# Feed-forward rows of a decoder block: the second norm's scale for the up rows applied at the output, product sums kept in PSUM, and the taps behind them

## What is computed

```python
hf = rmsnorm(x, norm_ffn_g[i])
g_pre = causal_dwconv(hf @ ffn_w_gate[i], ffn_conv_w[i], ffn_conv_b[i])
ff = (jax.nn.gelu(g_pre, approximate=False) * (hf @ ffn_w_up[i])) @ ffn_w_down[i]
x = x + ff
```

## Time and profile before

| | |
|---|---|
| median of 3 runs | 1895.88 us |
| the profiled execution | 1893.21 us |
| its span, first to last instruction | 1891.0 us |
| TensorE busy | 1804.0 us, 95% |
| VectorE busy | 1084.9 us, 57% |
| GpSimd busy | 871.9 us, 46% |
| ScalarE busy | 572.4 us, 30% |
| mean granted clock of TensorE | 0.990 |

### The profile page before, as it was taken

How to read it: one execution, slowest core, us unless ns; L and a number is a source line. 1 busy time by engine, 2 the same in 40 slices (tenths; PEclk the granted TensorE clock), 3 DMA queues, 4 the chain that set the end, 5 groups by cost and what they waited for, 6 DMA issues and landing times.

```text
span 1891.0 us, 24004 instructions
## 1 busy us (share of the span) xinstructions
PE 1804.0 (95%) x8628; PEld 1422.1 (75%) x8628; DVE 1084.9 (57%) x1531; ACT 572.4 (30%) x1095; POOL 871.9 (46%) x597
## 2 busy tenths in 40 slices
PE   7999999999999988999999999999999999999999
PEld 5777677767776766788788878777777777788887
DVE  5346644564654488344311333898888888943534
ACT  5542444344245423112311222523333333200000
POOL 7436443643543274563344433365556555322221
PEclk9999999999999999999999999999999999999999
DMA  4111211211121023445311144221112113145311
GB/s 168 34 40 40 59 49 40 62 51 40 40 56 45 23 68 90 113 112 174 105 67 67 67 167 167 100 101 67 67 67 92 74 67 111 57 177 210 112 44 56
DMA packets 64185, 157.99 MB, mean 84 GB/s; under 512 B 10912, under 2 KB 27680, under 8 KB 64112
## 3 DMA queue, kind: packets, MB, share of 16 engines
q1 hardware_dynamic: 51856, 145.35, 22.7%
q10 hardware_dynamic: 11792, 10.04, 2.0%
q0 software_dynamic: 464, 1.62, 0.2%
HBM read 123.54 MB, written 32.26 MB: 82 GB/s over the span
## 4 chain that ended last, share of the span: by engine, by line
PE 44%; DVE 22%; issue 18%; POOL 10%; ACT 3%; DMA 1%; DVEq 1%; POOLq 0%; SPq 0%; ACTq 0%
PE bank L899 7%; PE bank L900 7%; PE bank L901 7%; PE bank L1317 4%; PE bank L1319 4%; PE bank L1318 4%; POOL wlo L623 3%; DVE cv L2030 2%; PE bank L913 2%; PE bank L1047 2%; PE bank L1060 2%; PE bank L1033 2%; DVE st L2015 2%; DVE gbuf L2082 2%; DVE gbuf L2075 2%
## 5 line engine op out<-in xcount | busy, mean ns | idle before, releaser
L899 PE MATMUL bank<-hhi,whi 128*128 128x512 f32 x1024 | 421.4, 412 | 13.7 <-POOL wlo L623 8.0
L900 PE MATMUL bank<-hlo,whi 128*128 128x512 f32 x1024 | 404.8, 395 | 0.0
L901 PE MATMUL bank<-hhi,wlo 128*128 128x512 f32 x1024 | 404.6, 395 | 0.0
L623 POOL TENSOR_TENSOR wlo<-raw,whi 128x1024 fp32r<-128x1024 f32 (+1 forms) x84 | 196.6, 2340 | 236.6 <-DVE whi L1656 234.7
L899 PEld LDWEIGHTS bank<-hhi,whi 128*128 128x128 f32 x1024 | 193.7, 189 | 63.5 <-POOL wlo L623 10.4
L901 PEld LDWEIGHTS bank<-hhi,wlo 128*128 128x128 f32 x1024 | 193.4, 189 | 45.3
L900 PEld LDWEIGHTS bank<-hlo,whi 128*128 128x128 f32 x1024 | 194.0, 189 | 39.4 <-issue 1.2
L872 POOL TENSOR_TENSOR plo<-st,phi 128x512 fp32r<-128x512 f32 x60 | 108.3, 1819 | 50.2 <-ACT phi L1567 50.2
L1810 DVE CUSTOM_DVE_ANT_0 sp<-bank,mask 128x128 f32<-128x128 f32 (+1 forms) x192 | 56.1, 348 | 121.3 <-PE bank L1033 120.7
L1656 DVE CAST whi<-raw 128x1024 fp32r<-128x1024 f32 (+1 forms) x84 | 69.4, 826 | 93.3 <-PE bank L901 62.0
L1432 ACT ACTIVATE sp<-sp,negm 128x128 f32<-128x128 f32 (+1 forms) x192 | 83.8, 438 | 111.4 <-DVE negm L1814 111.4
(11 more groups left out here) (304 smaller groups left out, 4039.9 us busy)
## 6 DMA issues: line engine op xcount, KB each, us to landing
raw<-in_wblocks SPq DMA_DIRECT2D x98, 512.0 KB, 3.6
pair<-in_wblocks SPq DMA_DIRECT2D x40, 512.0 KB, 4.2
ff_scr<-ffo SPq DMA_DIRECT2D x22, 512.0 KB, 2.8
ff<-ff_scr SPq DMA_DIRECT2D x22, 512.0 KB, 4.1
rt<-rt_scr SPq DMA_DIRECT2D x8, 516.0 KB, 6.7
x<-in_xT SPq DMA_DIRECT2D x8, 512.0 KB, 8.7
zb_scr<-zb SPq DMA_DIRECT2D x8, 512.0 KB, 3.2
zb<-zb_scr SPq DMA_DIRECT2D x8, 512.0 KB, 3.3
```

The costliest lines, as they stand in the source:

```text
L623: pool.tensor_tensor(wlo[par][:, 0:cols], raw[par][:, 0:cols], whi[par][:, 0:cols].bitcast(F32), ALU.subtract).then_inc(lo_done, 1)
L899: nc.tensor.matmul(ps, a, x, start=start and k == k_list[0], stop=False)
L900: nc.tensor.matmul(ps, a, y, start=False, stop=False)
L901: last = nc.tensor.matmul(ps, b, x, start=False, stop=stop and k == k_list[-1])
```

## The change

Of the up rows, the factor rs1 is no longer applied to cv in each unit; each of the 16 output halves is multiplied by rs1 after the down projection, ahead of the residual. The results of four sums (C11, C12, C22, C21) are written back to the banks of the products that they read, and what follows reads them there. ScalarE no longer copies S1. The sums of S3 stand ahead of the taps on VectorE; ScalarE's tap stands behind the casts after S4 and waits for the second gate scaling (N_G1). ffo is made in two halves. TensorE waits for the first gate scaling ahead of A12 and for the whole end of the unit before (ff_done) ahead of S1. The banks of the down projection are taken in another order.

```diff
@@ -59,7 +59,8 @@
 NU = NF - 2
 SLOTS = 7
 I_A11, I_A12, I_S2, I_S1, I_S4, I_S3, I_A22 = range(1, SLOTS + 1)
-N_C11, N_U2, N_V, N_C12, N_U3, N_C22, N_C21 = range(1, SLOTS + 1)
+SUMS = 9
+N_C11, N_U2, N_G0, N_V, N_C12, N_G1, N_U3, N_C22, N_C21 = range(1, SUMS + 1)
 T_2, T_1, T_4, T_3 = range(4)
 B_11, B_12, B_21, B_22 = range(4)
 S_1, S_2, S_4, S_3 = range(4)
@@ -359,7 +360,7 @@
             return cws[:].rearrange("p (a b) c -> p b a c", b=2)[:, p, f2, :]
 
         def dbank(m, h):
-            return bank[(2 * m + h + 3) % 8]
+            return bank[(3, 4, 5, 6, 0, 1, 7, 2)[2 * m + h]]
 
         def half(ap, h):
             return ap[:, h * HT:(h + 1) * HT]
@@ -1274,19 +1275,20 @@
                 if first:
                     pe.wait_ge(ff_done, 2 + 4)
                 else:
-                    pe.wait_ge(copied, 2 * u)
-                    pe.wait_ge(cdone, SLOTS * u - SLOTS + N_C12)
+                    pe.wait_ge(copied, u)
                 product(I_A11, u, of_b(B_11))
+                if not first:
+                    pe.wait_ge(cdone, SUMS * u - SUMS + N_G0)
                 product(I_A12, u, of_b(B_21))
                 if first:
                     pe.wait_ge(tlo_done, KC // 2)
                 product(I_S2, u, of_t(T_2))
+                if not first:
+                    pe.wait_ge(ff_done, 2 * u + 8)
                 product(I_S1, u, of_t(T_1))
                 if first:
                     pe.wait_ge(gs_done, 2)
                 product(I_S4, u, of_b(B_22))
-                if not first:
-                    pe.wait_ge(cdone, SLOTS * u)
                 product(I_S3, u, of_t(T_3))
                 if first:
                     pe.wait_ge(ff_done, 4 + 4)
@@ -1308,10 +1310,11 @@
                             if free and c == 0:
                                 pe.wait_ge(out_ready, 2 * m + h + 1)
                             if start and not free and c == 0 and 2 * m + h == 1:
-                                pe.wait_ge(copied, 2 * NU)
-                                pe.wait_ge(cdone, SLOTS * (NU - 1) + N_C12)
+                                pe.wait_ge(copied, NU)
+                            if start and not free and c == 0 and 2 * m + h == 2:
+                                pe.wait_ge(cdone, SUMS * (NU - 1) + N_U3)
                             if start and not free and c == 0 and 2 * m + h == 6:
-                                pe.wait_ge(cdone, SLOTS * NU)
+                                pe.wait_ge(ff_done, 2 * NF + 4)
                             r = slice(c * HT + m * P, c * HT + (m + 1) * P)
                             x, y, ps = half(fhi[:, c, :], h), half(flo[:, c, :], h), dbank(m, h)[:]
                             nc.tensor.matmul(ps, dhi[par][:, r], x, start=start and c == 0, stop=False)
@@ -1554,7 +1557,6 @@
                 act.activation(thi[:, :, c, :], tbuf[c % 2][:].rearrange("p i (h t) -> p (i h) t", h=2), ACT.Copy).then_inc(thi_done, 1)
 
             def tap(f2, p):
-                act.wait_ge(gs_done, 2 * f2 + p + 1)
                 act.wait_ge(ff_done, 4 * f2 + 2 * p + 4)
                 w = conv_w(f2, p)
                 act.activation(cv[:], gbuf[:, p, 2:], ACT.Identity, scale=w[:, 2:3], bias=w[:, 3:4]).then_inc(tap_done, 1)
@@ -1583,17 +1585,14 @@
 
                 act.wait_ge(prod, SLOTS * u + I_A11)
                 if not first:
-                    act.wait_ge(cdone, SLOTS * u - SLOTS + N_U2)
+                    act.wait_ge(cdone, SUMS * u - SUMS + N_U2)
                 copy(s1_t[:], I_A11)
                 next_cast(I_A11)
                 next_cast(I_A12)
                 next_cast(I_S2)
-                act.wait_ge(prod, SLOTS * u + I_S1)
-                if not first:
-                    act.wait_ge(ff_done, 2 * u + 8)
-                copy(up_t[:, 1], I_S1)
                 next_cast(I_S1)
                 next_cast(I_S4)
+                act.wait_ge(cdone, SUMS * u + N_G1)
                 tap(i2 + 1, p)
                 next_cast(I_S3)
                 gelu(i2 + 1, p)
@@ -1608,6 +1607,7 @@
             rms(rs1, bank[2:4], 2)
             act.add_instruction(mybir.InstLoadActFuncSet(
                 name=nc.get_next_instruction_name(), engine=act.engine, act_func_set_id=GELU_SET))
+            act.wait_ge(gs_done, 1)
             tap(0, 0)
             t_scale(3)
             t_hi(3)
@@ -1617,6 +1617,7 @@
             act.wait_ge(pair_in[1], 32)
             cast(I_A11, 0)
             cast(I_A12, 0)
+            act.wait_ge(gs_done, 2)
             tap(0, 1)
             act.wait_ge(s_added, 4)
             cast(I_S2, 0)
@@ -2025,9 +2026,8 @@
                 link(V.scalar_tensor_tensor(cv[:], gbuf[:, p, 1:T + 1], w[:, 1:2], cv[:], ALU.mult, ALU.add))
                 V.scalar_tensor_tensor(cv[:], gbuf[:, p, 0:T], w[:, 0:1], cv[:], ALU.mult, ALU.add).then_inc(cv_done, 1)
 
-            def scaled(f2, p):
+            def activated(f2, p):
                 dve.wait_ge(gelu_done, 2 * f2 + p + 1)
-                link(TT(cv[:], cv[:], rs1[:], ALU.mult))
                 if not isinstance(f2, int) or f2:
                     dve.wait_ge(ff_out[p], 16 * f2)
 
@@ -2039,7 +2039,7 @@
                 last.then_inc(gs_done, 1)
 
             def up_evict(p):
-                scaled(0, p)
+                activated(0, p)
                 for h in range(2):
                     dve.wait_ge(groups, G_G + 4 * p + 2 + h + 1)
                     TT(half(ffo[p][:], h), half(cv[:], h), fbank(p, 1, h), ALU.mult).then_inc(ff_done, 1)
@@ -2048,14 +2048,19 @@
 
                 u = 2 * i2 + p
                 dve.wait_ge(prod, SLOTS * u + I_A22)
-                dve.wait_ge(cdone, SLOTS * u + N_C22)
-                TT(up_t[:, 0], up_t[:, 0], pbank(I_A22), ALU.add).then_inc(cdone, 1)
-                scaled(i2 + 1, p)
-                dve.wait_ge(cdone, SLOTS * u + N_C21)
-                TT(ffo[p][:], cv[:], up_t[:].rearrange("p h t -> p (h t)"), ALU.mult).then_inc(ff_done, 2)
+                dve.wait_ge(cdone, SUMS * u + N_C22)
+                TT(pbank(I_A22), up_t[:, 0], pbank(I_A22), ALU.add).then_inc(cdone, 1)
+                activated(i2 + 1, p)
+                TT(half(ffo[p][:], 1), half(cv[:], 1), pbank(I_S1), ALU.mult).then_inc(ff_done, 1)
+                dve.wait_ge(cdone, SUMS * u + N_C21)
+                TT(half(ffo[p][:], 0), half(cv[:], 0), pbank(I_A22), ALU.mult).then_inc(ff_done, 1)
 
             def unit(i2, p, first=False, last=False):
                 u = 2 * i2 + p
+
+                def added(n):
+                    dve.wait_ge(cdone, SUMS * u + n)
+
                 g = [gbuf[:, p, 2 + h * HT:2 + (h + 1) * HT] for h in range(2)]
                 if first:
                     up_evict(1)
@@ -2064,34 +2069,34 @@
                 if not last:
                     s_adds(i2 + p, 1 - p)
                 dve.wait_ge(prod, SLOTS * u + I_A12)
-                dve.wait_ge(copied, 2 * u + 1)
-                dve.wait_ge(cv_done, 2 * i2 + p + 1)
-                TT(g[0], s1_t[:], pbank(I_A12), ALU.add).then_inc(cdone, 1)
+                dve.wait_ge(copied, u + 1)
+                TT(pbank(I_A12), s1_t[:], pbank(I_A12), ALU.add).then_inc(cdone, 1)
                 dve.wait_ge(prod, SLOTS * u + I_S2)
                 if not first:
-                    dve.wait_ge(ff_done, 2 * u + 8)
+                    dve.wait_ge(cdone, SUMS * u)
                 TT(up_t[:, 0], s1_t[:], pbank(I_S2), ALU.add).then_inc(cdone, 1)
-                dve.wait_ge(cdone, SLOTS * u + N_C11)
-                link(TT(g[0], g[0], half(rs1[:], 0), ALU.mult))
+                added(N_C11)
+                dve.wait_ge(cv_done, 2 * i2 + p + 1)
+                TT(g[0], pbank(I_A12), half(rs1[:], 0), ALU.mult).then_inc(cdone, 1)
                 if last:
                     dve.wait_ge(ff_in[0], 32)
                     for x in range(2):
                         fsplit(0, 0, x, first=True)
-                dve.wait_ge(copied, 2 * u + 2)
-                dve.wait_ge(cdone, SLOTS * u + N_U2)
-                TT(g[1], up_t[:, 0], up_t[:, 1], ALU.add).then_inc(cdone, 1)
+                dve.wait_ge(prod, SLOTS * u + I_S1)
+                added(N_U2)
+                TT(up_t[:, 1], up_t[:, 0], pbank(I_S1), ALU.add).then_inc(cdone, 1)
                 if last:
                     hi_down(B_D, 0)
                 dve.wait_ge(prod, SLOTS * u + I_S4)
-                dve.wait_ge(cdone, SLOTS * u + N_V)
-                TT(g[1], g[1], pbank(I_S4), ALU.add).then_inc(cdone, 1)
-                dve.wait_ge(cdone, SLOTS * u + N_C12)
-                TT(g[1], g[1], half(rs1[:], 1), ALU.mult).then_inc(gs_done, 1)
-                conv(i2 + 1, p)
+                added(N_V)
+                TT(pbank(I_S4), up_t[:, 1], pbank(I_S4), ALU.add).then_inc(cdone, 1)
+                added(N_C12)
+                TT(g[1], pbank(I_S4), half(rs1[:], 1), ALU.mult).then_inc(cdone, 1)
                 dve.wait_ge(prod, SLOTS * u + I_S3)
```

(11 more changed lines are left out.)

## The result

The changed kernel takes 1864.71 us (median of 4 runs, 1863.58 to 1869.11), against 1895.95 of the kernel before beside it: ratio 0.984, 95% interval 0.982 to 0.9859. Measured again with the experiments it is 1866.34 against 1895.03, ratio 0.9849 (0.9834 to 0.9864). Forecast was 1867.8.

What follows compares the result with a forecast made beforehand. VectorE's loop with its tap wait set the 21.1 us units; after the change TensorE would bound at 19.35. Gains 34.1 + 2.4, losses 5.1 + 3.3: 28.1 us saved, 1867.8 us by the median; 8-in-10 range 1861 to 1882.

Steps and rivals of the forecast that it cites:

- Bound and units: The 20 units: TensorE would bound at 19.35 us each instead of 21.1, gaining 34.1 us in all.
- VectorE's loop: VectorE's work and waits per unit: predicted 17.9 us after the change, under TensorE's 19.35 by 1.4.
- Handoff: From last unit to down projection: the 2.59 us gap at the seventh bank would shrink, gaining 2.36 us, bounds 1.9 to 2.4.
- Evictions: Output halves after the down projection: 1.32 us each instead of 0.60, losing 5.1 us at the end, 3.3 in the middle.
- Sum: Whole kernel: 34.1 + 2.4 us gained, 5.1 + 3.3 lost, a saving of 28.1 us.
- Sums into PSUM: Four VectorE sums per unit that write PSUM banks: taken at 0.69 us each, bounds 0.6 and 1.72.
- rival B: Slower: VectorE sums writing PSUM are dear, 1.72 us each, lengthening the loop to 22.0; 1922 us, chance 0.04.
- cover of 1.4 us: Per unit, the margin by which VectorE's predicted 17.9 us stays under TensorE's 19.35.
- part (g): Output eviction: each of 16 halves becomes a PSUM product and a dependent sum; 5.1 and 3.3 us lost.
- A: Rival: VectorE's loop stays the bound in the units, but shorter, about 20.2 us; 1885 us, chance 0.12.
- D: Rival: the units' rhythm comes from something that stays, the stall moves to product S1; 1902 us, chance 0.03.
- C: Rival: output eviction is dear at 2.3 us a half, losing 24 in place of 8.4; 1883 us, chance 0.07.

## Why the prediction was right, point by point

- **Bound and units.** Foretold 19.35 us per unit and 34.1 gained; measured 19.33 and 34.6. That VectorE's loop against TensorE's own time decides, and not any one edit, is shown by the subsets: three different sets of edits (the change, the change with its scale left in, the change with its taps put back) all give units of 387 to 388 us in all, seven added products lengthen them to 442, three don't.
- **Handoff.** Foretold 2.4; measured 2.8 (245.1 us from first to last matmul of the down projection before, 242.3 without the output scale). The gap itself is the 2.36 that was read off it; two first steps of 0.1 more, behind the two waits of before, are also gone, and 0.2 is not placed.
- **Evictions.** 1.32 us per half was foretold and measured (1724.96 for the first, 1726.29 for the second, and so on). The end cost 5.2 (5.1 foretold). The middle cost 3.8 (3.3): its gaps are 3.2, and each restart of TensorE takes 0.1 longer for the first step.
- **Sum.** 34.6 + 2.8 - 9.0 = 28.4 from unit 0 on (671.1 - 642.8 in the spans), against 28.1. The single terms are up to 0.5 us off, and they cancel in part. The medians differ by 31.2 in one session and 28.7 in the other. What is beyond 28.4 the profiled executions don't show; the stretch ahead of unit 0 varies by more than that between executions, see below.
- **Sums into PSUM** read 0.69 each, the value taken; rival B with its 1.4 us or more is out. The Trainium skill's surcharge for a PSUM source ("VectorE: DVE Perf Modes", section "The TRN2 errata") is not seen here either: in the kernel after, line 2080 with a PSUM source reads 684 ns, line 2021 with two SBUF sources 692.
- **What was mis-sized: VectorE's loop.** 17.9 us foretold; it is 19.33 - 1.95 - 1.28 = 16.1. Two terms make most of it: s_adds 5.15 in place of 5.9, and the GELU, where 1.1 of waiting and the 0.7 sum beside it were both counted, and the waiting alone is 0.61. The terms as listed also add up to 17.7, not 17.9, and the smaller ones were each a little high. The error was on the safe side, so it didn't touch the forecast: the loop has only to be under 19.35. But with a cover of 1.4 us the 2.0 of the scale seemed too much to leave in the units. With the 3.2 that the trace of the kernel after shows it fits, and then part (g), 9 us of loss, bought nothing. That is the weak step: each edit was priced, and none was asked whether it was still needed beside the others.
- **Rivals.** A needed a loop over 19.35, D a rhythm from elsewhere; neither came. C's dear eviction didn't come: GpSimd has no row beside the first eviction (1724.96 to 1735.6) nor beside the second.

## What to carry to other kernels

Price a loop of helpers against the engine that should bound it, and stop cutting when it is under: every further cut gains nothing, and one that moves work to the tail or to a boundary is a loss (here 9 us, to be had back by leaving the scale in the units, 1858 us, or giving it to GpSimd, 1856). A cut on VectorE in a loop in which GpSimd works too needn't be worth its duration (2.04 us gave 1.1 here): look what slides beside what. Then add a known dose of work to find how much cover there is, since it tells in one run what a sum of rows only estimates.

## What the runs showed of the hardware

- VectorE operations with two SBUF operands took 0.68 to 0.69 us at 128x512 where GpSimd had nothing beside them, 1.78 beside its 128x512 subtractions (0.85 to 1.64 where they overlapped in part or in some units only) and 2.77 beside its 128x1024 multiplication. Those with a PSUM operand read 0.67 to 0.70 throughout. Moving the phase by 1.4 us switched line 2016 between 1.78 and 0.68. That taking 2.04 us out of the loop gave only 1.1, and adding 1.41 cost 0.15, was not expected.
- Some TensorE waits are followed by seven or eight matmul steps of 0.43 us in place of 0.23; the granted clock of the 7 us around such a place was 0.76, part of it at 1.2 GHz and the rest at 2.4. It happened behind waits of 1.9 (the handoff with three products), 2.0 (unit 1 with seven), 2.6 to 2.7 and 3.5 us. It did not behind the 2.2 us of the kernel before at its handoff, nor behind 2.0 in the kernel with only the scale moved, nor, from unit 0 on, behind any wait of 1.75 or less. So a wait of some 2 us may cost 1.4 to 1.6 us more than itself; what decides between the cases stays open.
- The stretch ahead of unit 0, the same code and work for TensorE in all twelve profiled executions, ends anywhere from 1219.2 to 1226.2 us. What sets this stays open. Compared from unit 0 to the end, the changed kernel's two executions agree to 0.01 us (642.75 and 642.76) while their spans differ by 3.3.
